# Modulation rows of the first norm alone made up front, the others inside a neighbourhood attention that runs scores two tiles ahead

## What is computed

```python
for i in range(DEPTH):
    mod_l = split(c_act @ mod_w[i] + mod_b[i], 6)        # shift, scale, gate of the mixer; shift, scale, gate of the experts
    mod_c = split(c_ctx_act @ mod_w[i] + mod_b[i], 6)
    hl = rms_norm(xl, norm_mix[i]) * (1 + mod_l[1]) + mod_l[0]
    hc = rms_norm(xc, norm_mix[i]) * (1 + mod_c[1]) + mod_c[0]
    yl, yc = neighbourhood_attention(hl, hc) if i == 0 else diff_attention(hl, hc)
    xl = xl + mod_l[2] * yl
    hl = rms_norm(xl, norm_ffn[i]) * (1 + mod_l[4]) + mod_l[3]
    ...                                                   # the same for xc in layer 0, grouped top-2 experts
    xl = xl + mod_l[5] * y
return rms_norm(xl, final_norm)
```

## Time and profile before

| | us |
|---|---|
| median of 3 runs (4432.39 to 4434.57) | 4434.53 |
| the profiled execution | 4424.82 |
| its span, first to last instruction | 4422.8 |
| TensorE busy in the span | 3919.2 (89%) |
| VectorE, ScalarE, GpSimd busy | 1172.5, 799.4, 497.6 |

### The profile page before, as it was taken

One profiled execution on the slowest core, in us unless ns is written; L12 is line 12 of the kernel. 1 busy time (PEld: TensorE's weight loads), 2 busy tenths in 40 slices (PEclk: granted clock), 3 DMA queues, 4 the chain that ended last, 5 costly groups with the idle time before them and its releaser, 6 DMA issues. The chain is left out here.

```text
span 4422.8 us, 55661 instructions
## 1 busy us (share of the span) xinstructions
PE 3919.2 (89%) x23164; PEld 2962.6 (67%) x23164; DVE 1172.5 (27%) x3113; ACT 799.4 (18%) x1768; POOL 497.6 (11%) x497
## 2 busy tenths in 40 slices
PE   5599999988949999999966999999988699999994
PEld 0266666664537789999844666666645589997873
DVE  2312222221221011111125555555533201111114
ACT  0123333331100000000012333333321000000001
POOL 0210000001420000000024111111013200000002
PEclk9799999998969999999988999999988799999997
DMA  9670000010155446778952000000102645579995
GB/s 371 185 305 24 19 24 19 19 48 25 43 180 171 134 151 214 247 261 277 311 194 65 14 16 15 15 15 15 44 15 78 206 162 194 193 249 310 311 308 171
DMA packets 469098, 621.06 MB, mean 140 GB/s; under 512 B 27136, under 2 KB 346128, under 8 KB 468728
## 3 DMA queue, kind: packets, MB, share of 16 engines
q1 hardware_dynamic: 440312, 521.58, 35.9%
q0 software_dynamic: 22240, 73.58, 4.6%
q10 hardware_dynamic: 6312, 22.45, 1.3%
HBM read 550.54 MB, written 67.40 MB: 140 GB/s over the span
## 5 line engine op out<-in xcount | busy, mean ns | idle before, releaser
L1610 PE MATMUL ps<-item_xT,expert_ring 128*128 128x128 f32 (+9 forms) x8192 | 1169.4, 306 | 1.1 <-DVE item_xT L1687 1.1
L1610 PEld LDWEIGHTS ps<-item_xT,expert_ring 128*128 128x128 f32 x8192 | 1115.6, 192 | 57.2 <-issue 5.7
L1643 PE MATMUL ps<-item_aT,expert_ring 128*128 128x144 f32 (+8 forms) x2304 | 409.1, 333 | 0.0
L1643 PEld LDWEIGHTS ps<-item_aT,expert_ring 128*128 128x128 f32 x2304 | 359.7, 193 | 25.3 <-issue 2.0
L1694 DVE TENSOR_TENSOR item_aT<-item_silu,ps 128x128 f32<-128x128 f32 (+9 forms) x256 | 83.8, 327 | 1069.2 <-ACT item_silu L1664 1069.2
L1664 ACT ACTIVATE item_silu<-ps 128x128 f32<-128x128 f32 (+9 forms) x256 | 79.1, 309 | 1314.9 <-PE ps L1610 1314.9
L683 PE MATMUL ps<-hT,w_group 128*128 128x512 f32 (+1 forms) x704 | 270.2, 527 | 0.4 <-PEq L301 0.4
L383 PE MATMUL ps<-hT,oT 128*128 128x512 f32 x576 | 254.5, 602 | 1.4 <-PEq L917 0.7
L1009 PE MATMUL ps<-hT,w_group 128*128 128x512 f32 (+1 forms) x576 | 232.4, 546 | 0.4 <-PEq L301 0.4
L1560 POOL DMA_INDIRECT gathered<-h_rows,slot_idx x55 | 52.6, 956 | 1531.2 <-PE ps L1593 1520.3
L1705 DVE COPY item_y<-ps 128x512 f32<-128x512 f32 (+3 forms) x106 | 69.0, 684 | 573.9 <-PE ps L1623 397.0
(11 more groups left out here) (207 smaller groups left out, 4223.5 us busy)
## 6 DMA issues: line engine op xcount, KB each, us to landing
expert_ring<-in_expert_w_gate SPq DMA_DIRECT2D x128, 1024.0 KB, 5.1
expert_ring<-in_expert_w_up SPq DMA_DIRECT2D x128, 1024.0 KB, 8.0
expert_ring<-in_expert_w_down SPq DMA_DIRECT2D x64, 2048.0 KB, 7.7
mod_ring<-in_mod_w SPq DMA_DIRECT2D x24, 2048.0 KB, 14.0
slot_out<-rows POOLq DMA_DIRECT2D x7, 4096.0 KB, 46.3
w_group<-in_w_qkv SPq DMA_DIRECT2D x48, 512.0 KB, 3.7
slot_out<-item_y ACTq DMA_DIRECT2D x35, 512.0 KB, 7.5
h_rows<-hr SPq DMA_DIRECT2D x18, 512.0 KB, 2.6
```

The costliest lines, as they stand in the source:

```text
L1610: m = nc.tensor.matmul(gub(j, b, w), ring[:, b // 2, k, w * 256 + (b % 2) * P:w * 256 + (b % 2 + 1) * P], xT[:, k, 0:C], start=k == 0, sto ...
L1643: m = nc.tensor.matmul(yb(j, d), ring[:, 4 + d // 4, f, (d % 4) * P:(d % 4 + 1) * P], aT[:, f, 0:C], start=f == 0, stop=f == FB - 1)
```

## The change

- `modulation` makes unit 0 alone, that is columns 0 to 2047 of layer 0 (shift and scale of the first norm). It loads them in four pieces of two rows a partition and 2048 columns (2 MB, runs of 8 KB), all issued at once; the four quarters of TensorE now hold the four 512-column parts of the unit, so no summing matmul is needed. `x` is loaded from ACT's queue, each load once a piece is in.
- The five other units of 2048 columns are made in the first two groups of the neighbourhood attention, in 20 pieces (two halves of 1 MB each, through a ring of three halves that lies in the part of `oT` not yet written). `modulate` is the last thing in each of the 20 steps on TensorE (PSUM bank 4, shared with the transposes), `add_piece` on DVE. Finished units are stored by SP in four small transfers; halves, weights, bias pieces and rows all go in SP's queue in program order.
- The attention runs one tile deeper: scores of tile i+2 in step i, behind a wait for the normalised probabilities of tile i+1 (`s_nm`). Step i is now values(i), scores(i+2), transposes(i+1) with its fifth block, the whole projection chunk, and in groups 0 and 1 the modulation piece. DVE multiplies the probabilities by the inverse sums before they are transposed (`normalised`), and `output` is a copy. `inverse_rows` and `take_inverse` are gone.

The diff, cut:

```diff
@@ modulation
-                W = sb(c, "mod_ring", [P, RING, KD, HALF])
+                W = sb(c, "mod_pieces", [P, 4, 2, UNIT])
+                acc = sb(c, "mod_rows", [P, HALF])
...
+                    src = a["mod_w"][0].rearrange("(p k) n -> p k n", k=KD)
+                    for n in range(4):
+                        sp.dma_start(W[:, n], src[:, 2 * n:2 * n + 2, 0:UNIT]).then_inc(w_in[n], 16)
+                    sp.wait_ge(s_rows, 1)
+                    unit_rows(sp, acc, 0, 0, s_out, True)
+                    sp.wait_ge(s_out, 64)
...
+                    for n in range(len(X_LOADS)):
+
+                        act.wait_ge(w_in[min(n + 1, 3)], 16)
+                        load_x(act, n)
...
+                    for k in range(KD):
+                        if k % 2 == 0:
+                            pe.wait_ge(w_in[k // 2], 16)
+                        for q in range(4):
+                            m = nc.tensor.matmul(bank(0)[q * QUART:(q + 1) * QUART, :], cq[:, k, :], W[:, k // 2, k % 2, q * HALF:(q + 1) * HALF],
+                                                 start=k == 0, stop=k == KD - 1)
@@ neighbourhood, SP
+                    def load_half(n):
+
+                        if n >= RING:
+                            sp.wait_ge(s_half, n - RING + 1)
+                        l, u = UNITS[n // 8]
+                        src = a["mod_w"][l].rearrange("(p k) n -> p k n", k=KD)
+                        sp.dma_start(ring[:, n % RING, :], src[:, n % 8, u * UNIT:(u + 1) * UNIT]).then_inc(h_in[n % RING], 16)
...
                     load_bias(0)
+                    for j in range(3):
+                        load_weights(1, j)
+                    for n in range(2):
+                        start_unit(n)
+                    for n in range(RING):
+                        load_half(n)
+                    for p in range(NPIECE):
+                        g, i = p // NS + 2, p % NS
+                        if i in (2, 5, 8):
+                            load_weights(g, i // 3)
+                        for n in (2 * p + RING, 2 * p + RING + 1):
+                            if n < 2 * NPIECE:
+                                load_half(n)
+                        if p % 4 == 0 and p:
+                            store_unit(p // 4 - 1)
...
@@ neighbourhood, TensorE
                     def scores(g, par, i):
                         t = order[i]
                         if i == 0:
                             pe.wait_ge(s_qk, g * NQK + NQK)
+
+                        pe.wait_ge(s_nm, g * 2 * NS + 2 * i)
...
+                    def modulate(g, i):
+
+                        p = g * NS + i
+                        pe.wait_ge(s_pT, g * NR + r0[i + 1] + 1)
+                        for n in (2 * p, 2 * p + 1):
+                            pe.wait_ge(h_in[n % RING], 16 * (n // RING + 1))
+                            for q in range(4):
+                                m = nc.tensor.matmul(bank(4)[q * QUART:(q + 1) * QUART, :], cq[:, n % 8, :], ring[:, n % RING, q * HALF:(q + 1) * HALF],
+                                                     start=n % 2 == 0, stop=n % 2 == 1)
+                            m.then_inc(s_half, 1)
...
                         for i in range(NS):
-                            if i + 1 < NS:
-                                scores(g, par, i + 1)
...
-                            fifths(g, i)
-                            inverse_rows(g, i, first)
-                            if i < NM and not last:
-                                project(g + 1, i, 0)
-                            values(g, par, i)
-                            if i < NM and not last:
-                                project(g + 1, i, 1)
+                            values(g, par, i, first)
+                            if i + 2 < NS:
+                                scores(g, par, i + 2)
                             elif not last:
-                                scores(g + 1, 1 - par, 0)
+                                scores(g + 1, 1 - par, i + 2 - NS)
+                            if mod and (g or i):
+
+                                pe.wait_ge(s_part, g * NS + i)
                             if i + 1 < NS:
                                 transposes(g, i + 1)
                             elif not last:
                                 transposes(g + 1, 0)
+                            if i < NM and not last:
+                                project(g + 1, i)
+                            if mod:
+                                modulate(g, i)
@@ neighbourhood, DVE
-                    def inverse(g, i):
+                    def normalised(g, i):
+                        w = len(near_keys(order[i])) * P
                         dve.wait_ge(s_exp, g * 2 * NS + 2 * i + 2)
                         nc.vector.reciprocal(rl[:, :], ls[:, :]).then_inc(s_rl, 1)
                         dve.wait_ge(s_rl, g * NS + i + 1)
                         for h in range(2):
-                            nc.vector.tensor_scalar(dg[:, h, :], ident, rl[:, h:h + 1], None, ALU.mult).then_inc(s_dg, 1)
+                            nc.vector.tensor_scalar(pb[:, i % 2, h, 0:w], pb[:, i % 2, h, 0:w], rl[:, h:h + 1], None, ALU.mult).then_inc(s_nm, 1)
...
@@ neighbourhood, ACT
                     def group(g, par, last=False):
                         for i in range(NS):
                             if i + 1 < NS:
-                                exps(g, i + 1)
...
-                            take_inverse(g, i)
...
+                            if i + 2 < NS:
+                                exps(g, i + 2)
+                            elif not last:
+                                exps(g + 1, i + 2 - NS)
```

More of the change, by code:

```diff
@@ L170, in build, with unit_rows @@
         ident = con[:, C_ID:C_ID + P]
+        QUART = 32
+        UNIT = 4 * HALF
+        cq = sb(top, "c_columns", [P, KD, QUART])
+        def unit_rows(eng, tile, l, u, done, store):
+            for q in range(4):
+                flat = slice(u * UNIT + q * HALF, u * UNIT + (q + 1) * HALF)
+                part = tile[q * QUART:q * QUART + 2, :]
+                if store:
+                    eng.dma_start(mods[l, :, flat], part).then_inc(done, 16)
+                else:
+                    eng.dma_start(part, a["mod_b"][l, flat].partition_broadcast(2)).then_inc(done, 16)
@@ L736, in transposes @@
                             m.then_inc(s_T, 1)
[L738 to L741 removed]
+                        if n > 4:
+                            if not first or i:
+                                pe.wait_ge(s_oT, g * NS + i)
                             for h in range(2):
@@ L793, in _ @@
                     scores(0, 0, 0)
-                    transposes(0, 0)
-                    group(0, 0, first=True)
-                    group(1, 1)
+                    transposes(0, 0, True)
+                    scores(0, 0, 1)
+                    group(0, 0, first=True, mod=True)
+                    group(1, 1, mod=True)
+                    pe.wait_ge(s_part, NPIECE)
                     with pe.Fori(1, GROUPS // 2 - 1) as gg:
@@ new lines, in add_piece @@
+                    def add_piece(p):
+                        n = p // 4
+                        if p % 4 == 0:
+                            dve.wait_ge(s_mb[n % 2], 64 * (n // 2 + 1))
+                        else:
+                            dve.wait_ge(s_part, p)
+                        dve.wait_ge(s_half, 2 * p + 2)
+                        nc.vector.tensor_tensor(acc[n % 2], bank(4), acc[n % 2], ALU.add).then_inc(s_part, 1)
+                        if p % 4 == 3 and n in scaled:
+                            m = scaled.index(n)
+                            dve.wait_ge(s_mgn[m % 2], 32 * (m // 2 + 1))
+                            dve.wait_ge(s_part, p + 1)
+                            half = slice(2 * QUART, P) if UNITS[n][1] == 0 else slice(0, 2 * QUART)
+                            v = acc[n % 2][half, :]
+                            nc.vector.scalar_tensor_tensor(out=v, in0=v, scalar=1.0, in1=gn[m % 2][half, :],
+                                                           op0=ALU.add, op1=ALU.mult).then_inc(s_unit, 1)
@@ L847, in group @@
                             if NQK <= i < NM and not last:
                                 take_values(g + 1, 1 - par, i, PROJ)
+                            if g * NS + i < NPIECE:
+                                add_piece(g * NS + i)
                     for n in range(NQK, NM):
                         take_values(0, 0, n, ahead_bank[n])
-                    biased(0, 0)
-                    inverse(0, 0)
+                    for i in range(2):
+                        biased(0, i)
+                        normalised(0, i)
```

210 lines of the change are left out of this document (90 added, 120 removed).

## The result

The kernel after takes 4279.14 us, the median of four runs (4274.65 to 4283.19), beside 4433.46 for the kernel before in the same session: a ratio of 0.9653 with a 95% interval of 0.9636 to 0.967. Predicted were 4298 and a range of 4260 to 4340. The profiled executions, one against the other, differ by 4424.82 - 4282.49 = 142.3 us where the sum said 136; the medians differ by 154.3. So of the 19 us between 4298 and 4279 some 13 come from the step from the profiled execution to the median (the kernel before ran 10 us under its median when profiled, the kernel after 3 over), and 6 from the sum. That the sum is so near hides errors of opposite sign, which the experiments separate.

A forecast was written before the change was run, and what follows sets the result against it. Modulation was taken as bound by DMA reads, attention by TensorE. Front -122, attention -69, pieces +33, +2 and +20 sum to -136: 4424.8 becomes 4289, plus 9.7 to the median gives 4298, range 4260 to 4340.

The forecast's parts named there:

- smooth: Rival, 4270 us: halves overtake the backlog (-12), boundaries at full clock (-6), x out of the way (-10); chance 0.15.
- the deeper order: Attention with scores two tiles ahead, without the modulation pieces: forecast -69 us (-55 to -80).
- Front, -122: Before the norm, 4 pieces of 2 MB read instead of 24: first norm instruction at 54 instead of 175.68 us.
- Start of the attention, +9.7: First tiles wait for normalised probabilities, so the first projection chunk starts at 278.3 instead of 268.56 us, old time.
- Pitch, 92.0: Time per attention group without modulation pieces: 92.0 us (90.5 to 94) instead of 99.65, six times, -45.9 us.
- C: Time from the end of a tile's scores to its normalised probabilities: 5.05 us (5.6 at 0.82 per scaling).
- the last group: Last attention group, without projection chunks: 60 us instead of 85.7, so -25.7 us.
- Pieces, +33 + 2 + 20: 20 modulation pieces in groups 0 and 1: matmuls +33 us, extra TensorE waits +2, late halves +20.
- M(0): First modulation piece in the attention; TensorE was to idle some 14 us there until both halves are in.
- clears first: Rival, 4328 us: halves get little beside the slot clears, TensorE waits in group 0, +50 instead of +20; chance 0.15.
- slower: Rival, 4521 us: scores two tiles ahead wait for the normalisation in every step, costing 220 us; chance 0.04.
- first P: First projection chunk of a group on TensorE; first to first was forecast 92 us apart in groups 2 to 6.

The follow-up runs named there:

- the run with the front alone: Old attention behind the new modulation stage making unit 0 alone, other rows copied: stretch from first projection to output projection 807.8 us, against 806.5 in the kernel before.
- the kernel with all three edits: Kernel after with slot clears behind group 3's bias tables, values' projection in four chunks, and scores waiting only for the bias pass: 4213.98 us, ratio 0.951.

## Why the prediction was right, and where it was not

**Sign and size.** Right: faster by 154 us, and 4279 lies in the range given (4260 to 4340), though 1 us below the forecast's own (4280 to 4316) and nearer to the number of "smooth" (4270) than to 4298. The traces show the mechanisms that the forecast names, with other sizes. That the sum of -136 came so near to -142 is in part luck: the deeper order gained 26 us more than forecast, the pieces cost 15.5 more, and the front gave 6 less.

**Front, -122.** Measured -119.6 at the first norm instruction. The single times were off (last piece 33.9 instead of 30, since x shares the engines from 17.9 us on; rows fetched at 47.5 instead of 40.5; first norm at 56 instead of 54, because nothing of the 5 us that I had added for x was needed: the fetch took 8.6 us, as before). What I had as two effects, pieces delayed and fetch delayed, is one amount of bytes, as the run with x held back shows. Of this gain 115.8 reach the attention. The norm's last part ran longer in this execution: 16.05 us for 32 matmuls of the first projections, which took 13.9 in the kernel before, 13.9 to 14.5 in ten of the runs above and 15.6 and 16.0 in two. The granted clock was 0.86 there, and 1.00 before; that I had not in the sum.

**Start of the attention, +9.7.** Measured 163.82 - 118.64 = 45.2 against 34.15, so +11.0; +9.3 in the run without pieces.

**Pitch, 92.0.** This is the term that was most mis-sized, six times over: 88.4 without pieces. (The six pitches before are 98.8 to 101.4 us, not equal; 99.65 is their mean.) C was right (4.9 us from the end of the scores at 505.75 to 510.66, for 5.05), so were the waits at the boundary (2.6) and the scaling of 128x640 in SBUF (551 ns for an estimate of 0.55):

```profile
L881 DVE TENSOR_SCALAR na_probs<-na_probs,na_suminv 128x640 f32<-128x640 f32 x96 | 48.8, 551 | 1.7
```

The Trainium skill, "VectorE: DVE Perf Modes", section "The perf-mode tier table", had such a scaling at twice the base rate, and this trace bears it out: 128 columns more cost 67 ns (484 ns at 512 columns), and 133 in the bias pass, which reads PSUM (689 and 822 ns). What I left out stands between the rows of a step: 11.40 - 10.65 = 0.75 us less, of which the removed L752 is only 0.37. A chunk in one go takes 513.86 - 506.89 = 6.97 instead of 3.64 + 3.53, 0.20 less, and the transposes with their fifth block right behind them 506.89 - 505.75 = 1.14 instead of 0.97 + 0.37, again 0.20. Both places have in common that a change from one kind of matmul to another is gone; that the change itself is what costs the 0.20 us is read from these rows alone, and no run tests it. It makes some 3 us of the 3.6 a group; the rest I put down, without a run of its own, to less half clock. Over six pitches the term is -67.6 instead of -45.9, in the seventh group -10.1 instead of -7.1, and -26.4 for the last group, where I had -25.7. (In the kernel after the last group took 55.1 us at a granted clock of 0.97, without pieces 60.0 at 0.87.)

**Pieces, +33 + 2 + 20.** Measured +70.5, of which +68.0 lie in groups 0 and 1 (131.9 and 111.5 us, where I had 110 to 125). The matmuls are 20 x 1.85 = 37, and the 3.9 us that I had taken off for two pieces in the boundary's gap were not to be had, for there they waited for their halves (2.65 and 2.71 us). The waits for halves are 24.2 us instead of 20: 17.6 at M(0) where I had 14, 0.8 at the half behind the weight piece where I had 5, and the boundary ones where I had 1. One wait of the values for the adding of a piece, 1.3. The remaining 8 us I attribute, by subtraction only, to half clock behind these waits. They are hardly more than the 5 us by which the stretch moves between executions: with the second execution of the kernel after (777.1, waits for halves 26.7) nearly nothing remains.

**The halves' share beside the clears.** I trusted the row that gave weight pieces 39 GB/s "little", and took 250 GB/s for the halves. The queues' packets (q0 is GpSimd's, q1 SyncE's) explain the row. From 118 to 150 us of the kernel after, and from 178 to 187, when the weight piece had landed:

```profile
q0 software_dynamic: 2466, 9.97, 77.9%
q1 hardware_dynamic: 2619, 1.28, 13.8%
```

```profile
q1 hardware_dynamic: 340, 2.37, 62.8%
q0 software_dynamic: 341, 1.36, 38.5%
```

Packets go nearly one for one: 2466 to 2619, then 341 to 340. The clears' packets are 9.97 MB / 2466 = 4.0 KB, not the 2 KB of their runs as I had assumed, so that 512 bytes win a ninth, 40 of 353 GB/s, which is the row. By the Trainium skill, "DMA: Bandwidth & Descriptors", section "Queues, rings and completion order", each engine takes its queues in turn, a packet each; the equal counts of the trace agree, with its own packets of 512 bytes, 4 KB and 8 KB as the unit, and it was my packet size that was wrong. The halves get 2.37 MB in 9 us, 263 GB/s, as I had taken, but only from 177 us on, when the weight piece has landed (149.21 + 28.1). Until then that piece, issued ahead of them, drains at 512 bytes to the clears' 4 KB: from 171 to 177 us SyncE's 376 packets carried 0.36 MB, the clears' 480 packets 1.96 MB. The rival "clears first" had the right cause with too high a price. "Smooth" was refuted by M(0)'s wait, by the half clock at the boundaries and by x, which was not out of the way; its halves in time came only when the clears were moved (756.2).

**The offset.** I carried the 9.7 us between the profiled execution and the median over to the kernel after. That was the largest part of the miss of the number: 13 of 19 us. Single executions of the kernel after lie between 4270.6 and 4286.0, so one profiled execution says nothing about the side on which the median lies. One small sum was off too: the rival "slower" adds 220 us to 4298, which is 4518 and not 4521.

## What to carry to other kernels

The deeper order paid more than the waits that it took away. Count a step from row to row, not instruction by instruction, and the rest is seen: 0.75 us a step here, where the removed instruction accounts for 0.37. A wait that is added on the bounding engine costs only where the chain exceeds the work beside it; look for the steps with least work (group boundary, last group), and let the instruction wait for what it needs and no more: a chunk in every step and the right semaphore were worth 21 to 29 us each here. Bulk transfers that nobody waits for belong behind the ones that somebody does, in time and not only in another queue, since beside 4 KB packets a stream of 512-byte packets got a ninth here (40 of 353 GB/s), and a weight piece took 28.1 us to land instead of 3.7, with the halves behind it.

## What the runs showed of the hardware that was not expected

- Issuing on SyncE slows under the backlog: ten transfers of 4 KB took 20.3 us beside the clears and 3.1 without them, and six bias pieces 20.32 and 14.33 us where the free queue took 3.73. It is not the clears alone: with the halves first the same ten took 6.7 us beside them, when fewer small packets stood ahead in SyncE's own queue. A weight piece of 512 KB landed after 28.1 us beside the clears and after 3.7 without.
- In every kernel TensorE has, at one boundary (that of groups 3 and 4), one or two waits of 1 to 3 us which no engine and no transfer ends ("issue" in the trace: 2.76 and 1.36 us at 580 us in the kernel after). With the old attention there is one of 2.43 us at 548 us in the run with the front alone. It is the place where TensorE's loop over groups 2 to 5, two groups a round, jumps back. The DMA records show packets of 16 KB of the kind "instruction" there close together, at 577.6, 580.8 and 585.4 us, while in the groups before they are 13 to 26 us apart; TensorE stands from 577.7 to 580.4 and from 582.0 to 583.4. In the kernel with all three edits they start at 529 to 530 and 533 to 534, with the waits from 530.8 to 532.5 and 533.6 to 536.2. That points to code being loaded at the jump; the records do not name the engine, and no run tested it, so the cause stays open. Group 3's pitch (92.0 us) is some 3 us longer than its neighbours' (89.0 us) with it.
- Between executions of the same kernel the stretch moved from 782.2 to 777.1 us, although the second waited 2.5 us longer for halves. What differs are the places at which matmuls ran at half clock: from group 2's first P to group 3's, for instance, 87.5 us (402.39 to 489.93) instead of 89.1.
